# A two-layer diffusion trunk on one core: the layer loop written out, the semaphore clears dropped, the next layer's first steps moved into the expert block

## What is computed

```
Each layer:
  h  = RMSNorm(x) * (1 + scale1) + shift1
  x += gate1 * W_out( sum_b sigmoid(G_b h) * Branch_b(h) )      three mixers A, B, C
  h  = RMSNorm(x) * (1 + scale2) + shift2
  x += gate2 * MoE(h)             16 experts, top-1 group of 4, top-2 experts inside it
shift/scale/gate = SiLU(cond) @ W_ada[l] + b_ada[l]

def modulation(cvec, w, b):
    m = jax.nn.silu(cvec) @ w + b
    return m.reshape(m.shape[:-1] + (6, D_MODEL))
```

## Time and profile before

| | us |
|---|---|
| median of 3 runs | 2784.48 |
| lowest and highest run | 2783.02, 2785.20 |
| the profiled execution, own time | 2785.75 |
| its span, first to last instruction | 2783.9 |
| TensorE busy (matmul) | 2454.4, 88% |
| VectorE, ScalarE, GpSimd busy | 893.8, 510.1, 106.0 |
| TensorE's mean granted clock, share of full | 0.927 |
| DMA moved | 440.60 MB, 158 GB/s on the mean |

### The profile page before, as it was taken

The page is one execution under the profiler, slowest core; times in us unless marked ns, Lnnn a source line. Parts: engine busy times, 40 slices in busy tenths (PEclk is TensorE's granted clock), DMA queues, the critical chain, the costliest instruction groups (busy, mean ns, idle before and its releaser), DMA issues. The chain is left out here.

```text
span 2783.9 us, 39618 instructions
## 1 busy us (share of the span) xinstructions
PE 2454.4 (88%) x16902; PEld 1508.4 (54%) x16902; DVE 893.8 (32%) x1492; ACT 510.1 (18%) x906; POOL 106.0 (4%) x74
## 2 busy tenths in 40 slices
PE   6999999889899969999479999997898999599893
PEld 3546654554576545555245476555545765455552
DVE  2255312431558130000113562224315661300002
ACT  1133202210223021010021241022102220201000
POOL 0000000000021000000000000001001110000000
PEclk8999999899989979999789999898999899699996
DMA  6321132114314277999353201411243222799972
GB/s 241 106 93 61 54 140 93 46 61 151 125 32 146 91 297 272 376 373 345 115 184 112 93 31 62 165 61 46 71 159 117 89 78 91 298 346 379 375 272 80
DMA packets 162338, 440.60 MB, mean 158 GB/s; under 512 B 10150, under 2 KB 50086, under 8 KB 153448
## 3 DMA queue, kind: packets, MB, share of 16 engines
q1 hardware_dynamic: 144360, 412.75, 40.6%
q10 hardware_dynamic: 14336, 12.59, 1.5%
q0 software_dynamic: 3456, 12.58, 1.2%
HBM read 400.38 MB, written 37.52 MB: 157 GB/s over the span
## 5 line engine op out<-in xcount | busy, mean ns | idle before, releaser
L293 PE MATMUL ps<-space 128*128 128x384 f32 (+3 forms) x1696 | 475.5, 433 | 14.9 <-DVE space L469 8.5
L293 PE MATMUL ps<-hT,space 128*128 128x384 f32 x1344 | 461.3, 504 | 27.3 <-ACT hT L407 12.1
L293 PEld LDWEIGHTS ps<-space 128*128 128x128 f32 x1696 | 300.1, 194 | 187.7 <-issue 48.4
L293 PEld LDWEIGHTS ps<-hT,space 128*128 128x128 f32 x1344 | 262.0, 197 | 213.4 <-issue 41.4
L1673 PE MATMUL ps<-space 128*32 128x256 f32 x6144 | 343.7, 384 | 1.7 <-ACT space L1783 1.5
L293 PE MATMUL ps<-space,hT 128*128 128x512 f32 x768 | 336.7, 599 | 3.8 <-PEq L1191 3.8
L1673 PEld LDWEIGHTS ps<-space 128*32 128x32 f32 x6144 | 201.9, 111 | 133.8 <-issue 12.6
L293 PEld LDWEIGHTS ps<-space,hT 128*128 128x128 f32 x768 | 146.9, 192 | 192.0 <-issue 191.4
L1694 PE MATMUL ps<-space 128*32 128x256 f32 x3072 | 184.2, 398 | 1.5 <-DVE space L1915 1.5
L325 PE MATMUL ps<-cst,space 128*128 128x128 f32 x492 | 84.6, 324 | 90.5 <-DVE space L1927 29.8
L1694 PEld LDWEIGHTS ps<-space 128*32 128x32 f32 x3072 | 100.9, 115 | 74.2 <-issue 15.8
(11 more groups left out here) (255 smaller groups left out, 2262.7 us busy)
## 6 DMA issues: line engine op xcount, KB each, us to landing
space<-in_e_w SPq DMA_DIRECT2D x96, 2048.0 KB, 15.2
space<-in_w_in SPq DMA_DIRECT2D x36, 2048.0 KB, 8.5
space<-in_w_ada SPq DMA_DIRECT2D x24, 2048.0 KB, 8.2
h_rows<-space SPq DMA_DIRECT2D x2, 6144.0 KB, 25.7
space<-h_rows SPq DMA_DIRECT2D x32, 384.0 KB, 17.9
y_rows<-mT ACTq DMA_DIRECT2D x128, 96.0 KB, 10.4
space<-in_a_wo SPq DMA_DIRECT2D x4, 2048.0 KB, 11.4
space<-in_b_wo SPq DMA_DIRECT2D x4, 2048.0 KB, 8.2
```

The costliest lines, as they stand in the source:

```text
L293: ins = pe.matmul(out, a, b, start=(i == 0), stop=(i == len(pairs) - 1))
```

## The change

- The loop on the engines becomes a Python loop, so the program holds the code of both layers, with constant addresses. `clear_counts` goes with all its calls. Semaphores count on through the program: thresholds of layer l are raised by the number of counts of the layers before (`RING_LOADS`, `MOE_LOADS`, factors of `l + 1`).
- The overflow block goes. Its work stands as four functions inside the expert block, at the end of the experts and ahead of the use of the gathered rows, behind the same test of the flag, with semaphores of its own for each layer. The flag's writing gets a semaphore (`flag_ready`).
- In the expert block of the first layer SP loads the next layer's parameters behind the first tokens, the next layer's ring chunks 0 to 2 behind the last expert weights, and four more chunks as the modulations free the ring. PE and DVE run the four modulations between the last expert and the sum of squares, and the three engines run the first norm at the end of that block.
- For the first layer the same work moves into the program's first block.

```
-        with nc.Fori(0, DEPTH) as l:
+        for l in range(DEPTH):
+            ring_layer[0] = l
...
                 @block.tensor
                 def _(pe):
-                    for n in range(ADA_FIRST):
-                        if n == 2:
-                            square_sum(pe, "n1", sq_x, KD)
-                        modulation_pe(pe, n)
-                    for n in range(ADA_FIRST):
-                        modulation_features_pe(pe, n, mod_rows[:, n, :])
                     pe.wait_ge(*following(pe, "h_ready", 2))
                     feature_major(pe, W_CQ, "cq", hT)
...
                 @block.sync
                 def _(sp):
-                    for dst, src in ((vec[:, :], vecs), (row[:, :], rows)):
-                        sp.dma_start(dst, ...).then_inc(sem["params_in"], 16)
...
-                    load_weights(sp, l, RING, W_BV + 2)
+                    load_weights(sp, l, RING + ADA_FIRST, W_BV + 2)
```

The first block:

```
                 pe.wait_ge(sem["xin"], 64)
                 to_features(pe, "x", x_in)
+                pe.wait_ge(*following(pe, "cond_ready"))
+                modulation_pe(pe, 0)
+                square_sum(pe, "n1", mT, KD)
+                for n in range(1, ADA_FIRST):
+                    modulation_pe(pe, n)
+                for n in range(ADA_FIRST):
+                    modulation_features_pe(pe, n, mod_rows[:, n, :])
...
                 load_weights(sp, 0, 0, RING)
+                load_params(sp, 0)
+                load_weights(sp, 0, RING, RING + ADA_FIRST)
                 sp.wait_ge(sem["xin"], 64)
...
-        clear_counts()
```

The end of the expert block, on PE, SP, ACT and DVE:

```
                     output_pe(NE - 1)
+                    pe.wait_ge(*following(pe, "flag_ready"))
+                    overflow_pe(pe)
+                    ring_layer[0] = l + 1
                     for t in range(NT):
+                        if not last:
+                            for n in ((0, 1), (2,), ())[t]:
+                                modulation_pe(pe, n)
                         for q in range(2):
                             pe.wait_ge(*following(pe, "y_summed"))
                             transposed(pe, ("moe", t, q), ...)
+                    if not last:
+                        modulation_pe(pe, 3)
+                        for n in range(3):
+                            modulation_features_pe(pe, n, mod_rows[:, n, :])
+                        square_sum(pe, "n1", sq_m, KD)
+                        modulation_features_pe(pe, 3, mod_rows[:, 3, :])
...
-                    sp.wait_ge(scattered, 16 * 2 * NT)
+                    sp.wait_ge(scattered, 16 * 2 * NT * (l + 1))
                     for e in range(2):
                         load_tokens(e)
+                    sp.wait_ge(*following(sp, "flag_ready"))
+                    if not last:
+                        load_params(sp, l + 1)
                     for e in range(NE):
                         sp.wait_ge(*made(("up", e)))
...
+                    if not last:
+                        for n in range(RING):
+                            m = N_W - MSLOTS + n
+                            sp.wait_ge(*made(("y" if m % 3 == 2 else "up", m // 3)))
+                            load_weights(sp, l + 1, n, n + 1)
+                    overflow_sp(sp)
+                    if not last:
+                        load_weights(sp, l + 1, RING, RING + ADA_FIRST)
...
                     output(NE - 1)
+                    act.wait_ge(*following(act, "flag_ready"))
+                    overflow_act(act)
                     for t in range(NT):
-                        act.wait_ge(y_back[t], 32)
+                        act.wait_ge(y_back[t], 32 * (l + 1))
...
+                    if not last:
+                        norm_act(act, 0, "n1", sq_m, [("moe", t, q) for t in range(NT) for q in range(2)])
...
+                    overflow_dve(dve)
                     for t in range(NT):
+                        if not last:
+                            for n in ((0, 1), (2,), ())[t]:
+                                modulation_rows_dve(dve, n, mod_rows[:, n, :])
                         for q in range(2):
                             dve.wait_ge(*following(dve, "y_scaled"))
...
+                    if not last:
+                        modulation_rows_dve(dve, 3, mod_rows[:, 3, :])
+                        dve.wait_ge(*following(dve, "params_in", 64))
+                        for n in range(3):
+                            modulation_dve(dve, n)
+                        root_mean(dve, "n1", D)
+                        modulation_dve(dve, 3)
+                        amplitude(dve, 0, V_N1)
+                        norm_dve(dve, 0)
-            clear_counts(loads=True)
...
-            clear_counts()
```

Each overflow function has one form; `load_params` holds the four loads that stood in the layer's first block:

```
+            def overflow_act(act):
+                with act.If(act.value_load(overflow[0:1, 0:1], min_val=0, max_val=1) > 0):
+                    with act.Fori(0, NE) as e:
...
```

More of the change, by code:

```diff
@@ L87 @@
 QD = D // 4
+B_HID, B_OUT, N_OUT = 0, 4, 3
+OVER_BANKS = B_OUT + N_OUT
+RING_LOADS = 20
+MOE_LOADS = 6
 GRP = 32
@@ L148, in trunk_kernel @@
         last_use = {}
+        ring_layer = [0]
         def counts(name):
@@ L397, in amplitude, with norm_act @@
             dve.wait_ge(*counted("dve_step"))
-        def norm_act(act, i, key, sq):
+        def norm_act(act, i, key, sq, made_from=()):
+            for k in made_from:
+                act.wait_ge(*read(k))
             act.activation(sq, xT[:, :, :], ACT.Square).then_inc(*counts("squares_ready"))
@@ L481, in project_pe, with load_params @@
                     between()
+        mod_rows = carve(20480, ADA_FIRST, 512)
         x_in = carve(0, NT, D)
+        def load_params(sp, l):
+            for dst, src in ((vec[:, :], vecs), (row[:, :], rows)):
+                sp.dma_start(dst, src[bass.ds(l, 1)].rearrange("a p n -> p (a n)")).then_inc(sem["params_in"], 16)
+            sp.dma_start(wsm[:, :, :], kpn(w_small, l)).then_inc(sem["params_in"], 16)
+            sp.dma_start(wgl[:, :, :], w_gate_low[bass.ds(l, 1)].rearrange("a r d n -> r (a d) n")
+                         ).then_inc(sem["params_in"], 16)
         with nc.Block() as block:
@@ new lines, in overflow_sp @@
+            def overflow_sp(sp):
+                with sp.If(sp.value_load(overflow[0:1, 0:1], min_val=0, max_val=1) > 0):
+                    sp.wait_ge(*made(("y", NE - 1)))
+                    for i in range(3):
+                        src, k, w = expert_source(i, l, 0)
+                        sp.dma_start(over_matrix(i), src).then_inc(ov_loaded[i], 16)
+                    with sp.Fori(1, NE) as e:
+                        for i, b in enumerate((B_HID + 2, B_HID + 3, B_OUT + N_OUT - 1)):
+                            sp.wait_ge(ov_full[b], e * 2 + 1)
+                            src, k, w = expert_source(i, l, e)
+                            sp.dma_start(over_matrix(i), src).then_inc(ov_loaded[i], 16)
```

251 lines of the change are left out of this document (114 added, 137 removed).

## The result

The changed kernel takes 2757.01 us, the median of 4 runs (2745.15 to 2762.35), the kernel before beside it 2784.56 (4 runs, 2783.02 to 2785.20). The medians are 27.6 us apart; the ratio is 0.9897, interval 0.9877 to 0.9917, so 23 to 34 us are won. The forecast was 34.2 us won and 2750.3; the range of 2738 to 2764 holds the result. The profiled execution is the fastest of the four, 2745.15.

The account below looks back on a forecast made before the run. TensorE is busy 2454 of 2784 us, so only gaps at end, start and layer boundary can be won: -15.0 + 1.8 - 21.0 = -34.2 us, giving 2750.3, range 2738 to 2764.

Parts of the forecast that it names:

- The end: Program end, last xT update to next product: 15.67 us becomes 0.67, 15.0 won, without clearings and overflow block.
- The start: Program start to first product on hT: 1.8 us lost, from -0.4 cache load, +1.5 cold fourth modulation, +0.7 block boundary.
- The upper bound for slow feature products: Program start: if the small feature products run slow too, 4.87 us against 3.73, the loss is +2.9 instead of +1.8.
- The boundary: Between the layers: 21.0 us won, 30.0 from work moved ahead of the last xT update less 9.0 for later xT.
- B: Layer boundary from the last xT update to the first product on hT: 20.9 us in place of 50.95.
- A: Layer boundary from the last output product's end to the last xT update: 9 us longer, 8.0 gather, one DVE.
- The lower bound for that coupling: Layer boundary: with gather undisturbed, DVE's copy of the third modulation alone delays xT by 2.8 us, 1370.9 against 1368.1.
- the estimate by that rule: Layer boundary, queues taking turns: gather of 16.6 us from 1359.9, 11.5 us delay with DVE's one, total 2753.
- Rival 1: Start gains its 5.6 us and the boundary's gather is undisturbed: 47.8 us won, 2737; chance 0.12.
- Rival 2: Layer boundary: weights issued first starve the gather, delay 17 to 20 us, 2759 to 2762; chance 0.17.
- Rival 3: Second layer's block entries and overflow skips: code not yet run makes it slower, past 2784.5, 2805 at 5 us each; chance 0.03.
- Rival 4: Layer boundary: early work brings nothing, weights' landing replaces jump and clearings; within 5.6 us of before; chance 0.02.

Follow-up runs that it names:

- e4: The changed kernel with the overflow test and its path left out on all four engines; 2753.54 us, ratio 0.9893.
- e5: The kernel before with only its layer loop written out in Python, clearings, overflow block and late loads kept; 2783.46 us, ratio 0.9989.
- e9: The changed kernel with its start undone, the first layer's modulations and norm back in that layer's first block; 2758.15 us, ratio 0.9905.
- e11: The changed kernel with ring loads in SP's expert loop, third modulation before transposes, projection chunks behind the gather, fourth chunk before parameters at the start; 2750.30 us.
- e1: The changed kernel run again, unedited; 2761.13 us, ratio 0.9913.
- e3: The changed kernel with the three ring loads issued inside SP's expert loop as slots come free; 2753.67 us, ratio 0.9892.
- e6: The changed kernel with nothing of the next layer begun early: loads, modulations and norm in the next layer's first block; 2770.12 us, ratio 0.995.
- e7: The changed kernel with ring loads inside SP's expert loop, and the next layer's modulations and norm in its first block; 2752.13 us, ratio 0.9881.
- e2: The changed kernel with early loads kept, but the next layer's modulations and norm back in its first block; 2752.70 us, ratio 0.9903.

## Why the prediction was right, and where it was off

**The end: predicted -15.0, measured -13.7.** The gap became 0.53 us instead of 15.67 as worked out. The missing 1.3 are the overflow test: "over 8 us cover the test" looked only at ACT's next wait, but POOL's gather waits for ACT's last stores to land, and with the test in the program the last of them lands 0.7 to 1.9 us later (e4). e5 keeps the 42.2, so the clearings and their blocks are the whole gain. By the Trainium skill (Runtime: NRT & Kernel Launch, Instruction fetch mechanics) a taken branch to a target outside the pages at hand waits for a fetch. The trace agrees: TensorE's pause at the skip, 2.9 to 5.7 us and none in e4, ends 1.7 us behind a 16 KB packet of the instruction queue in all seven kernels in which a modulation waits there.

**The start: predicted +1.8, measured +1.65, and +4.5 to +5.0 in four of the nine executions with this start.** The low clock's modulation was predicted at 3.40 and took 3.48, the first product was predicted at 49.0 and came at 48.84. That +1.65 lies so near +1.8 is in part luck: the mean of the nine executions is +3.2. The upper bound for slow feature products, +1.1, was too small: they cost 3.3 (6.99 against 3.73), since the whole of them can run at 1.2 GHz. The boundary's +0.7 is +0.4 (e9). The lower bound, a landing 2.5 us earlier, was not given by the change but could be had by moving one load (e11).

**The boundary: predicted -21.0, measured -20.6 (-19.1 in e1).** Both of its parts held. B was predicted at 20.9 and is 20.1, the sum of squares 6.80 (8.38 in e1) against 7.4. A was predicted 9 us longer and is 10.2 longer. Inside A the prices differ: stores land in 6.1 us, not 8.1, so the gather starts 4.8 us later and not 6.2; the last of the six gathers takes 11.4 us instead of 6.0, which makes the other 5.4. The third modulation's copy on DVE, put at 1 us, costs nothing here (0.5 us in e3): from the last gathered row to the last xT update it is 9.04 us in both kernels. That so many shifts sum to nearly the predicted 9 is in part luck. The lower bound for that coupling is also added up wrong by 0.2: its terms give 1370.7, not 1370.9. The DMA windows of after, where in before the DMA share was 0.17 to 0.49 from 1338 to 1358:

```profile
1337.00:1347.00 10.00, 9.26 (x168) 6.00 (x163) 0.56 (x1) 0.81 (x1) 0.00 (x0) 1.00 1.01 368
1347.00:1357.00 10.00, 4.36 (x28) 1.13 (x24) 0.24 (x1) 0.81 (x1) 0.00 (x0) 0.76 0.92 343
1357.00:1367.00 10.00, 2.62 (x16) 0.45 (x8) 1.14 (x2) 0.26 (x1) 5.71 (x6) 0.67 0.94 342
```

By the Trainium skill (DMA: Bandwidth & Descriptors, Queues, rings and completion order) queues with work take turns at each engine; the estimate by that rule was a gather of 16.6 us and a delay of 11.5, DVE's one among them. The trace agrees: these are the queues of the gather and of the weights from 1359.7 to 1374.8, with packets, MB and share.

```profile
q0 software_dynamic: 864, 3.15, 52.8%
q1 hardware_dynamic: 1449, 2.93, 50.8%
```

Each moved about half of the bytes, and from the first gather's issue to the last one's landing it is 17.7 us (1357.12 to 1374.82). Without DVE's one the rule's delay is 10.5, nearer to the measured 10.2 than the 8 of the sum of bytes, which had gather and weights end together.

**The sum: predicted -34.2, measured -27.6.** The touched stretches give -32.6 in one execution and -28.7 in e1. What was mis-sized is the start, whose slow feature products cost some 3 us in nearly half of the executions, then the test, 1.3. What is left is the inner stretches: 2596.8 to 2615.2 in the twelve kernels from after on that are unrolled and have no clearings, 2608.5 on their mean, against 2605.8 in the one execution of before and 2603.6 in e5. In them TensorE is idle for 207.2 us on the mean and in before for 210.4; busy it is for 2401.3 and 2395.4, with a granted clock in mixers 0 of 0.929 to 0.934 against 0.939, in mixers 1 of 0.928 to 0.939 against 0.939. So on the mean the change added no wait there, and the excess is products at a lower clock. Whether the change lowers that clock stays open, with one traced execution of before. Nothing speaks for the parameters' load at 1045 us: experts 0 take 298.8 in after, and 302.6 in e6, which does not load there.

**The rivals.** Rival 1, an undisturbed gather and 5.6 us won at the start, fell: A grew by 10, and the start lost. Another order of loads gives the undisturbed gather (e7), but only 0.9 us at the start (e11, 46.3 against 47.2). Rival 2, starvation, fell at 10 us of delay instead of 17; its times are 1 us too long by its own sum, which gives 2758 to 2761. Rival 3 fell: mixers and experts take 1298.2 us in layer 1 and 1298.6 in layer 0, and over the twelve kernels the difference goes from -3.8 to +7.7 with no direction. The sign that was set for it, a second layer over 1336 us, is just reached in e3 (1336.6), at a granted clock of 0.928 in mixers 1. Rival 4 describes e5. It doesn't describe e6, which begins nothing early and still wins 13.9 us by its ratio of 0.995, more than the 5.6 that rival 4 allows.

What the four parts of the boundary bring, going from before to after in this order: loop written out -4.2 (77.2 to 73.0), clearings and blocks -4.6 (68.4), early loads -11.5 (56.9), early modulations and norm -0.4 (56.5). The last step is smaller than what B scatters by, and with the ring's loads well placed it is +0.4 (e7 to e3). The part with the most code brings nothing that can be told from none.

## What to carry to other kernels

Removing a barrier or a pause wins only what nothing else was hiding in it: name the load that had been landing meanwhile, and start it earlier (e6 against e2, 11.5 us). Before filling an idle stretch with work, ask what that work must load and which small transfers on whose landing the chain waits (stores, gathers) it will stand beside; here the moved computation won 5.8 us and its loads took 5.4. And place each load in the issuing engine's order by its own release and its own user, since a load behind another one's wait is late by that wait.

## What was not expected of the hardware

- The same 32 products of two columns took 4.10 or 6.99 us in different executions of the same program, at 2.4 or 1.2 GHz, after about the same pause (6.87 and 7.14 us) and the same work; and between after and e1 products at another granted clock moved the inner stretches by 11 us.
- A DMA issue on SP held its engine for 4.57 to 5.23 us while earlier loads were still moving, where the same issue took 0.37 and 0.43 in the kernel before, which came to it at 21.4 us with the three chunks nearly through. The fourth chunk was issued at 23.26 us for that reason, and not only because its turn comes late in the code. That the queue was full is my reading; no run shows its fill.
- One load of 2 MB beside six gathers raised them from 5.5 to 9.2 us; four loads did no worse (9.4).
- TensorE's skip over the overflow code left 5.55 to 5.67 us idle in after, e1 and e9, with the DMA engines busy, and 2.94 to 3.43 in the kernels whose ring loads were already through. The packet of code that it waits for takes no longer in after than in e3 (1.0 us both); it begins 2.6 us later. What holds it back no run tells.
